# A first norm whose squares and scale go through TensorE: eight chunks and eight condition tiles moved off VectorE

## The reference

```python
c_act = jax.nn.silu(c)
mod = c_act @ w_ada[l] + b_ada[l]
sh1, sc1, g1, sh2, sc2, g2 = [m[:, None, :] for m in jnp.split(mod, N_MOD, axis=-1)]
h = rmsnorm(x, norm1_g[l]) * (1.0 + sc1) + sh1
proj = h @ w_in[l]
```

## Time and profile before

| quantity | value |
|---|---|
| median of 3 runs | 2550.76 us (2548.2 to 2552.28) |
| the profiled execution, its time | 2547.89 us |
| its span | 2546.0 us |
| TensorE matmul busy | 2346.5 us, 92% |
| VectorE busy | 1093.0 us, 43% |
| mean granted TensorE clock | 0.968 |

### The profile page before, as it was taken

How to read it: one execution, slowest core, us unless ns; L and a number is a source line. 1 busy time by engine, 2 the same in 40 slices (tenths; PEclk the granted TensorE clock), 3 DMA queues, 4 the chain that set the end, 5 groups by cost and what they waited for, 6 DMA issues and landing times.

```text
span 2546.0 us, 30718 instructions
## 1 busy us (share of the span) xinstructions
PE 2346.5 (92%) x11230; PEld 1945.6 (76%) x11230; DVE 1093.0 (43%) x1334; ACT 770.9 (30%) x1077; POOL 856.7 (34%) x851
## 2 busy tenths in 40 slices
PE   4797888989999999999988988989999999999996
PEld 3585777777888888888777777877778888888885
DVE  7766888459641344134454252343211112222233
ACT  3226776122220222024324353453112111112210
POOL 1254554325333333323322231322223333333331
PEclk9897999989999999999998999999999999999998
DMA  5411000623111111111131110102001111111131
GB/s 229 174 45 34 17 16 10 247 99 148 68 49 50 50 49 46 45 66 45 37 136 36 52 54 16 62 8 81 29 29 49 50 46 53 49 45 46 48 117 74
DMA packets 46009, 165.96 MB, mean 65 GB/s; under 512 B 4224, under 2 KB 6016, under 8 KB 44800
## 3 DMA queue, kind: packets, MB, share of 16 engines
q1 hardware_dynamic: 45952, 165.19, 18.7%
HBM read 156.79 MB, written 8.39 MB: 65 GB/s over the span
## 4 chain that ended last, share of the span: by engine, by line
PE 71%; issue 12%; DVE 7%; POOL 4%; ACT 3%; DMA 2%; SPq 0%; DVEq 0%; ACTq 0%; POOLq 0%
PE acc L657 64%; PE bank L900 1%; DVE ADA L1348 1%; POOL EX L586 1%; DMA WF<-in_w 1%; DVE acc L1488 1%; POOL WL L512 1%; PE bank L755 1%; ACT EX L1078 1%; POOL WH L510 1%; PE bank L943 1%; DVE HL L1334 1%; PE bank L940 1%; PE turn L888 1%; DVE CV L1329 0%
## 5 line engine op out<-in xcount | busy, mean ns | idle before, releaser
L657 PE MATMUL acc<-HH,WH 128*128 128x512 f32 x1792 | 557.1, 392 | 10.6 <-POOL WL L512 10.1
L657 PE MATMUL acc<-HL,WH 128*128 128x512 f32 x1792 | 554.0, 391 | 0.0
L657 PE MATMUL acc<-HH,WL 128*128 128x512 f32 x1792 | 553.6, 390 | 0.0
L509 POOL TENSOR_TENSOR WH<-WF,CON 128x16 fp32r<-128x16 f32 x186 | 52.4, 282 | 1305.4 <-PE acc L657 1111.9
L512 POOL TENSOR_TENSOR WL<-WF,WH 128x1024 fp32r<-128x1024 f32 (+2 forms) x186 | 440.5, 2368 | 15.5
L657 PEld LDWEIGHTS acc<-HH,WH 128*128 128x128 f32 x1792 | 337.0, 189 | 84.1 <-issue 8.1
L657 PEld LDWEIGHTS acc<-HL,WH 128*128 128x128 f32 x1792 | 337.9, 189 | 70.7
L657 PEld LDWEIGHTS acc<-HH,WL 128*128 128x128 f32 x1792 | 337.8, 189 | 70.6
L1594 DVE SCALAR_TENSOR_TENSOR CV<-EV,VEC,CV 128x1023 f32<-128x1023 f32 x44 | 104.5, 2374 | 205.2 <-ACT CV L1147 204.8
L510 POOL TENSOR_SCALAR WH<-WF 128x1008 fp32r<-128x1008 f32 (+2 forms) x186 | 187.9, 1010 | 0.0
L1546 DVE SCALAR_TENSOR_TENSOR XT<-acc,MOD,XT 128x1024 f32 (+1 forms) x40 | 51.3, 1284 | 270.4 <-PE acc L657 270.4
(11 more groups left out here) (308 smaller groups left out, 3754.8 us busy)
## 6 DMA issues: line engine op xcount, KB each, us to landing
WF<-in_w SPq DMA_DIRECT2D x150, 512.0 KB, 3.5
ADA<-in_ada SPq DMA_DIRECT2D x15, 1024.0 KB, 14.8
BIAS<-in_bias SPq DMA_DIRECT2D x8, 1152.0 KB, 5.1
XT<-in_xT SPq DMA_DIRECT2D x16, 512.0 KB, 9.8
ADA<-in_ada SPq DMA_DIRECT2D x4, 2048.0 KB, 11.5
ADA<-in_ada SPq DMA_DIRECT2D x3, 2560.0 KB, 9.4
WF<-in_w SPq DMA_DIRECT2D x24, 256.0 KB, 2.6
ADA<-in_ada SPq DMA_DIRECT2D x8, 512.0 KB, 3.4
```

What stands on the lines that cost most here:

```text
L509: pool.tensor_tensor(h[:, 0:FEW], f[:, 0:FEW], zero.to_broadcast([P, FEW]), ALU.add).then_inc(w_hi, 1)
L657: last = pe.matmul(acc[:, slot, HALF * c:HALF * c + HALF], w[slot][:, k, :], x[:, k, HALF * c:HALF * c + HALF], start=(k == 0 and w is WH ...
```

## The change

TensorE takes over two jobs, and VectorE's program for the first norm is put in another order.

- The chunks' squares are no longer added by VectorE. `first_stats` opens an accumulation with a product of zeros, and then runs eight matmuls for each chunk as its square is ready: 64 instead of eight.
- The scale tiles of `w_ada` are stored untransposed, and `scale_of(k)` forms the eight-fold product on TensorE with the condition as eight columns (`CCOLS`, from a new entry of `VEC`, with a Silu of its own on ScalarE). It runs for k = 0 ahead of `spread_rs`, and for k = 1 to 7 inside `first_pair`, ahead of the wait for chunk k - 1.
- VectorE keeps the shifts (`first_shift`). Two are computed first, then one in each chunk; `first_scale` forms `A1` straight from PSUM, and the reciprocal comes behind the first of them.

```diff
-            def first_pair(n, q, context=None):
+            def first_pair(n, q, context=None, ahead=None):
...
                 for k in range(KD - 1):
+                    if ahead is not None:
+                        ahead(k + 1)
                     pe.wait_ge(hh_ready, q * KD + k + 1)
...
+            def first_stats():
+
+                pe.matmul(bank6[:, 0:TT], ident, zero.to_broadcast([P, TT]), start=True, stop=False)
+                for k in range(KD):
+                    pe.wait_ge(sq_ready, k + 1)
+                    for t in range(TT):
+                        mm = pe.matmul(bank6[:, t:t + 1], SQ1[:, k, P * t:P * t + P], one, start=False,
+                                       stop=(k == KD - 1 and t == TT - 1))
+                mm.then_inc(stat_done, 1)
+
+            def scale_of(k):
+
+                pe.wait_ge(ada1_in[k], 16)
+                w = ADA1[k // 2][:, 2 * (k % 2) + 1, :]
+                for i in range(KD):
+                    mm = pe.matmul(bank7[:, k:k + 1], w[:, P * i:P * i + P], CCOLS[:, i:i + 1],
+                                   start=(i == 0), stop=(i == KD - 1))
+                mm.then_inc(scale_done, 1)
+
             pe.wait_ge(consts_in, 32)
-            stats(0, SQ1[:, 0, :])
+            first_stats()
+            pe.wait_ge(ccols_ready, 1)
+            scale_of(0)
             spread_rs(0)
...
-            first_pair(N_IN, 0)
+            first_pair(N_IN, 0, ahead=scale_of)
...
             act.wait_ge(consts_in, 32)
+            act.activation(CCOLS[:, :], vec("c", 0, KD), ACT.Silu).then_inc(ccols_ready, 1)
...
-            for k in range(1, KD):
-                dve.wait_ge(sq_ready, k + 1)
-                ins = dve.tensor_tensor(SQ1[:, 0, :], SQ1[:, 0, :], SQ1[:, k, :], ALU.add)
-                if k < KD - 1:
-                    link(ins)
-            ins.then_inc(sq_summed, 1)
-            dve.tensor_copy(MX[:, 5:6], eps).then_inc(sq_used, KD)
-
-            invert(0)
+            dve.wait_ge(consts_in, 32)
+            dve.tensor_scalar(MOD1[:, KD:2 * KD], vec("b_ada", KD, KD), 1.0, None, ALU.add).then_inc(sq_used, KD)
+            dve.wait_ge(sq_used, KD)
+
+            def first_shift(k):
+
+                dve.wait_ge(ada1_in[k], 16)
+                modulation(ADA1[k // 2][:, 2 * (k % 2), :], C1A, MOD1[:, k:k + 1], used=2)
+                link(dve.tensor_copy(MX[:, 6:7], eps))
+                steps.did(dve.tensor_tensor(MOD1[:, k:k + 1], MOD1[:, k:k + 1], vec("b_ada", k), ALU.add))
+
+            def first_scale(k):
+                dve.wait_ge(scale_done, k + 1)
+                dve.scalar_tensor_tensor(out=A1[:, k:k + 1], in0=bank7[:, k:k + 1], scalar=MOD1[:, KD + k:KD + k + 1],
+                                         in1=vec("norm1_g", k), op0=ALU.add, op1=ALU.mult).then_inc(mods_ready, 1)
+
             dve.wait_ge(cond_ready, 1)
+            first_shift(0)
+            first_shift(1)
             for k in range(KD):
-                dve.wait_ge(ada1_in[k], 16)
-                for b in range(2):
-                    modulation(ADA1[k // 2][:, 2 * (k % 2) + b, :], C1A, MOD1[:, KD * b + k:KD * b + k + 1])
-                link(dve.tensor_copy(MX[:, 6:7], eps))
-                both, biases = MOD1[:, k:KD + k + 1:KD], vec("b_ada", 0, 2 * KD)[:, k:KD + k + 1:KD]
-                link(dve.tensor_tensor(both, both, biases, ALU.add))
-                dve.scalar_tensor_tensor(out=A1[:, k:k + 1], in0=MOD1[:, KD + k:KD + k + 1], scalar=1.0,
-                                         in1=vec("norm1_g", k), op0=ALU.add, op1=ALU.mult).then_inc(mods_ready, 1)
+                first_scale(k)
+                if k == 0:
+                    invert(0)
+                    dve.wait_ge(rb_done, 1)
                 dve.wait_ge(mods_ready, k + 1)
-                if k == 0:
-                    dve.wait_ge(rb_done, 1)
+                steps.settle()
                 normed_chunk(0, k, A1[:, k:k + 1])
                 if k > 0:
                     normed_second(0, k - 1, MOD1[:, k - 1:k])
+                if k + 2 < KD:
+                    first_shift(k + 2)
             normed_second(0, KD - 1, MOD1[:, KD - 1:KD])
```

More of the change, by code:

```diff
@@ L80 @@
          ("b_ada_2", 24), ("norm_g_2", 8), ("b_in_2", 64), ("w_conv_2", 12), ("b_conv_2", 4), ("final_g_2", 8),
-         ("q_norm_g", 1), ("k_norm_g", 1)]
+         ("q_norm_g", 1), ("k_norm_g", 1), ("c", 8)]
 VCOL, NVEC = {}, 0
@@ L239, in build @@
         RC = at("RC", small + 1.5, [P, 8])
+        CCOLS = at("CCOLS", small + 1.5, [P, KD])
         DG = [at(f"DG{s}", small + 1.625 + 0.5 * s, [P, P]) for s in range(2)]
@@ L274, in build @@
         sq_summed, stat_done = sem("sq_summed"), sem("stat_done")
-        mods_ready = sem("mods_ready")
+        mods_ready, ccols_ready, scale_done = sem("mods_ready"), sem("ccols_ready"), sem("scale_done")
         sqh_ready, qstat_done, rot_done, kms_done = sem("sqh_ready"), sem("qstat_done"), sem("rot_done"), sem("kms_done")
@@ L662, in stats @@
             def stats(q, sums):
-                pe.wait_ge(sq_summed, q + 1)
+                pe.wait_ge(sq_summed, q)
                 for t in range(TT):
@@ L1344, in normed, with modulation @@
                 normed_second(q, KD - 1, shift(KD - 1))
-            def modulation(w, cond, out):
+            def modulation(w, cond, out, used=1):
                 ins = dve.scalar_tensor_tensor(out=w, in0=w, scalar=1.0, in1=cond[:, :], op0=ALU.mult, op1=ALU.mult, accum_out=out)
-                ins.then_inc(ada_used, 1)
-            for k in range(1, KD):
-                dve.wait_ge(sq_ready, k + 1)
-                ins = dve.tensor_tensor(SQ1[:, 0, :], SQ1[:, 0, :], SQ1[:, k, :], ALU.add)
-                if k < KD - 1:
-                    link(ins)
@@ L1357, in _ @@
-            ins.then_inc(sq_summed, 1)
-            dve.tensor_copy(MX[:, 5:6], eps).then_inc(sq_used, KD)
-            invert(0)
+                ins.then_inc(ada_used, used)
+            dve.wait_ge(consts_in, 32)
[6 more added lines that the diff above has]
+                steps.did(dve.tensor_tensor(MOD1[:, k:k + 1], MOD1[:, k:k + 1], vec("b_ada", k), ALU.add))
@@ L1837, in layout @@
         "q_norm_g": np.concatenate([f["q_norm_g"][0]] * 2)[:, None],
-        "k_norm_g": np.concatenate([f["k_norm_g"][0]] * 2)[:, None],
+        "k_norm_g": np.concatenate([f["k_norm_g"][0]] * 2)[:, None], "c": cols_of(f["c"].reshape(-1)),
     }
@@ L1865, in layout @@
     ada = np.concatenate([f["w_ada"][0].T, f["w_ada_2"][0].T]).reshape(72, P, D)
-    ada = ada[[c for k in range(KD) for c in (k, KD + k)] + list(range(2 * KD, 72))]
+    scale1 = tiles_of(f["w_ada"][0][:, D:2 * D])
+    first = [w for k in range(KD) for w in (ada[k], scale1[k])]
+    ada = np.concatenate([np.stack(first), ada[2 * KD:]])
     conds = np.ascontiguousarray(np.stack([np.broadcast_to(f[k].reshape(1, D), (P, D)) for k in ("c", "c_2", "c_ctx_2")]))
```

## The result

The changed kernel takes 2566.12 us in the median of 4 runs (2561.11 to 2568.33), against 2550.16 us of the kernel before on the same chip: 1.006 times as long, interval 1.0042 to 1.0077, so 11 to 20 us slower. The forecast was 2571 us in a range of 2563 to 2586. On another chip the same pair gave 2571.09 against 2547.69 us, 1.0086 (1.0073 to 1.0099).

The account below looks back on a forecast made before the run. VectorE's chunk chain was taken to bound the first 70 us. Late statistics, first factor and a TensorE-ordered loop put the eighth factor 20.2 us later: 2550.8 + 20.2 = 2571 us on the median, range 2563 to 2586.

Parts of the forecast that it names:

- Statistics: First norm's sums on TensorE: 128 one-column records at 0.213 us, low clock, ending at 36.1 us, 13.6 us late.
- the fast rows: Two-column matmuls behind dense work on TensorE: loads of 192 ns, 0.107 us a record, read as the 2.4 GHz price.
- First factor and spread: After the statistics: first scale ends at 39.5 us, then factor, reciprocal and transposes, from 40.0 to 42.0 us.
- The two early shifts: VectorE's first two shift products, 2.5 us begun around 20 us, hidden behind the statistics.
- The loop: TensorE's HH, HL, scale order: two low periods of 8.54 and four high of 5.55, 39.3 us; eighth factor at 84.9.
- The high period: One chunk of the changed loop at 2.4 GHz: scale 1.71, the larger of 2.83 and HH, HL 0.91, 0.1: 5.55 us.
- 5.27 us, eight times: VectorE's time for one chunk in the loop of the kernel before, said to occur eight times.
- Behind the loop: Everything behind the eighth factor shifts one for one; tile 2 still starts 21.4 us behind COS.
- rival (c): Shift partly absorbed before tile 2, perhaps 5 to 10 us coming back: 2563 us; chance 0.05.
- Rival (a): Low clock through the whole loop, six periods of 8.54 us, +32.1 us: 2583 us; chance 0.12.
- Rival (d): VectorE's shorter program gains 1.15 us in each of eight chunks, TensorE's work free: 2541.6 us; chance 0.01.
- Rival (b): The long run of small statistics matmuls raises the clock by itself, 1.3 us earlier: 2549.5 us; chance 0.08.

Follow-up runs that it names:

- the dense start: Changed kernel plus three dense matmuls on TensorE ahead of the statistics: 2564.40 us against 2547.72 of the kernel before, ratio 1.0059.
- two scales early: Both steps, plus chunk 0's scale on VectorE, scales 1 and 2 run early, later ones three chunks ahead, reciprocal before shifts: 2542.35 us, 0.9978 of the kernel before.
- the statistics alone: Kernel before with the 64 statistics matmuls on TensorE, both condition products still on VectorE: 2559.53 us against 2547.72, ratio 1.0042.
- both steps: Changed kernel with sums of squares back on VectorE and scale k + 2 between HH and HL of chunk k: 2546.31 us, 1.0000 of the kernel before.
- the order tests: Changed kernel with scale k + 2 between HH and HL of chunk k: 1.0034 of the kernel before; both steps: 1.0000; two scales early: 0.9978.
- the sums back on VectorE: Changed kernel with sums of squares returned to VectorE, scales kept on TensorE: 2554.43 us against 2547.72 of the kernel before, ratio 1.0026.

## Why the prediction was right, point by point

**Statistics.** 128 records at 0.213 us, end forecast at 36.1, measured 8.62 + 27.47 = 36.09. What decided it was to price them at the low clock, by the granted 0.50 at 546 us and not by the fast rows; the dense start shows the same price where the trace grants 0.50. The Trainium skill ("TensorE: Matmul & The Clock Gate", section "Why this matters for your kernels") advises to keep TensorE busy to get the full clock. For one-column matmuls the trace with the dense start does not agree: 5.00 of 5.00 us busy at 0.50.

**First factor and spread.** Forecast 42.0, measured 41.89. The factor itself took 0.22 us, not 0.16. Its reading from PSUM does not explain that: in the kernel with two scales early, chunk 0's factor reads `SUM` instead of the bank and takes 0.22 us too. What both have and the kernel before has not is a column (`MOD1`) in place of the constant 1.0; no run tests whether this is the cause. The two early shifts were put at 2.5 us from about 20 us on; they ran from 22.98 to 28.66, which stayed hidden behind the statistics.

**The loop.** Six periods were forecast as 39.3 us; from the second scale's end at 45.09 to the eighth factor at 84.77 it is 39.7. The sum is right, its make-up less so, and that it came this close is partly luck: the same loop took 3.8 us less behind the dense start. I had two periods wholly at the low clock and four at the high one, and the factors of the changed kernel are 6.9, 6.3, 7.1, 6.1, 7.3 and 5.9 us apart: the clock changes within nearly every period. The high period is 5.70 and not 5.55. The prediction's "5.27 us, eight times" for the kernel before is a misreading that its sum does not use: there are seven intervals between eight factors, and the first is 4.06 us (28.55 to 32.61), since no HL stands in it. The expectation for the statistics alone took seven of 5.27 and put COS half a microsecond too late.

**Behind the loop.** Forecast: COS to tile 2 stays 21.4. Measured 21.45 after, so nothing was absorbed and rival (c) falls. Over the experiments it is 20.3 (both steps) to 21.6 us (two scales early), so a shift of COS passes on to within about 1 us, not exactly. Rival (a), a low clock throughout, would have been COS at 96.8. Rival (d), a free gain, falls by the time, and the order tests show why: a gain appeared only in the kernel whose TensorE has scales ready ahead.

**Rival (b)** falls by the clock, but its price was also too low. It lets the spread end at 28.1 us and says that early statistics would let the first chunk start no later than 28.75. With the sums back on VectorE, where the statistics are early, it started at 30.77: the reciprocal stands behind the first factor, and that waits for the two early shifts.

**What was mis-sized.** The median came out 16.0 us slower on its chip and 23.4 on the other, with 20.2 forecast. The profiled executions put COS at 85.0 and 84.5 in the two. From tile 2 to the end the ten profiled executions have between 2457.6 and 2463.3 us, and the changed kernel itself 2459.9 in one and 2463.1 in the other. The two profiled executions of the first chip differ by 2568.33 - 2547.89 = 20.4 us, the forecast almost exactly. The prediction has the spread between executions in its range and not in its sum, and took it as that of the kernel before, 4 us. The traces show two places where it arises: the unchanged rest with its nearly 6 us, and the changed loop itself with 3.8. Which of them makes the medians 16.0 and 23.4 stays open, since the other executions have no trace.

## What to carry to other kernels

Matmuls with one column cost their weight loads (PEld, the loads, was busy for 27.38 of the 27.47 us). A long run of them was at the low clock here, throughout where TensorE came to it idle and from 13 us on where it came from dense work: price them at 0.21 us a record before you take sums away from an engine that was idle anyway. When work moves into an in-order engine that already has a chain with another one, its place counts beside its length: the same 16 records, 1.7 us long, cost 1.14 us less per chunk (4.56 instead of 5.70) between the two dense groups than ahead of both. Moving work off the bounding engine paid here only in the kernel where the other engine had results in store.

## What was not expected of the hardware

The granted clock reads 1.00 from the start of the span in both first traces, though the loads last 333 ns and wide pairs are 0.85 us apart. In the trace with the dense start, whose clock changed early, the same stream reads 0.50. The column seems to show full clock until the first change is recorded, so durations have to be read beside it.

Pieces of VectorE became long beside GpSimd's weight split. In the changed kernel:

```profile
24.05 3.19 POOL L513 TENSOR_TENSOR WL<-WF,WH 128x1024 fp32r<-128x1024 f32 x1
...
25.15 2.11 DVE L1386 TENSOR_TENSOR MOD<-MOD,VEC 128x1 f32<-128x1 f32 x1
...
28.50 0.16 DVE L1386 TENSOR_TENSOR MOD<-MOD,VEC 128x1 f32<-128x1 f32 x1
```

An addition of one column took 2.11 us and ended with the split (27.26 and 27.24), and 0.16 us a chunk later. The condition product ahead of it took 2.06 us, where those without a split take 1.22. The split became longer too: with the statistics alone, where VectorE is idle at that time, it took 2.34 us instead of 3.19. With the sums back on VectorE the same two pieces are 2.06 and 2.11 us, some 2.8 more than alone, and this put its first factor at 28.4, where the scale was done at 26.3.
